# Gated DeltaNet inside a two-layer trunk: the key and query products of a block made once for both directions, and kept in SBUF by ScalarE

## What is computed

```python
# per chunk and head; qn, kn are L2-normalised; forward and backward directions are summed
gc = cumsum(g); decay = exp(where(i >= j, gc_i - gc_j, -inf))
lower = where(i > j, (k_i * b_i) . k_j * decay, 0)         # key x key
sol   = solve(I + lower, [v * b, k * b * exp(gc)])          # u, w
intra = where(i >= j, q_i . k_j * decay, 0)                 # query x key
v_new = u - w S
o     = (q * exp(gc)) S + intra v_new
S     = S * exp(g_last) + (k * exp(g_last - g))^T v_new
# o = o_fwd + flip(o_bwd of the flipped sequence)
```

## Time and profile before

| | |
|---|---|
| median of 3 runs | 2117.73 us (2115.81 to 2118.25) |
| profiled execution, its time | 2117.53 us |
| its span, first to last instruction | 2115.7 us |
| mean granted TensorE clock | 0.969 |
| busy: TensorE / weight load / VectorE / ScalarE / GpSimd | 94% / 88% / 50% / 31% / 21% |
| recurrence of the first layer | about 404 to 537 us |
| recurrence of the second layer | about 1433 to 1566 us |

### The profile page before, as it was taken

One profiled execution on the slowest core, in us unless ns is written; L12 is line 12 of the kernel. 1 busy time (PEld: TensorE's weight loads), 2 busy tenths in 40 slices (PEclk: granted clock), 3 DMA queues, 4 the chain that ended last, 5 costly groups with the idle time before them and its releaser, 6 DMA issues. The chain is left out here.

```text
span 2115.7 us, 33396 instructions
## 1 busy us (share of the span) xinstructions
PE 1990.3 (94%) x14407; PEld 1871.7 (88%) x14407; DVE 1059.3 (50%) x1666; ACT 664.4 (31%) x1009; POOL 446.5 (21%) x326
## 2 busy tenths in 40 slices
PE   5999979899899999999999998898979999999996
PEld 3999957788899999999999988587879999999996
DVE  3445886577652323323455478666775332333232
ACT  2543225412223131312335422552122313122231
POOL 4000010133243030312430000103323412122144
PEclk9999989999899999999999998999989999999998
DMA  8444120100333222122254431101012212221211
GB/s 330 160 161 152 41 66 1 36 1 1 115 131 109 80 100 80 61 80 80 70 201 160 145 108 61 25 2 36 1 55 80 81 64 77 80 80 61 80 61 50
DMA packets 45635, 177.89 MB, mean 84 GB/s; under 512 B 21073, under 2 KB 22865, under 8 KB 26033
## 3 DMA queue, kind: packets, MB, share of 16 engines
q1 hardware_dynamic: 43952, 174.29, 23.5%
q10 hardware_dynamic: 1536, 1.48, 0.2%
HBM read 166.98 MB, written 8.68 MB: 83 GB/s over the span
## 5 line engine op out<-in xcount | busy, mean ns | idle before, releaser
L1416 PE MATMUL PS<-HH,HI 128*128 128x322 f32 (+1 forms) x1792 | 420.4, 316 | 4.5 <-DVE HL L939 4.5
L1416 PE MATMUL PS<-HL,HI 128*128 128x322 f32 (+1 forms) x1792 | 415.2, 313 | 0.0
L1416 PE MATMUL PS<-HH,LO 128*128 128x322 f32 (+1 forms) x1792 | 414.2, 312 | 0.0
L603 ACT CAST HI<-RAW 128x2048 fp32r<-128x2048 f32 x96 | 182.8, 1904 | 514.0 <-PE PS L1416 478.8
L1416 PEld LDWEIGHTS PS<-HH,HI 128*128 128x128 f32 x1792 | 303.3, 191 | 8.8 <-issue 8.7
L1416 PEld LDWEIGHTS PS<-HH,LO 128*128 128x128 f32 x1792 | 306.1, 191 | 0.0
L1416 PEld LDWEIGHTS PS<-HL,HI 128*128 128x128 f32 x1792 | 305.2, 191 | 0.0
L1416 PE MATMUL PS<-FH,HI 128*128 128x320 f32 x1280 | 293.3, 310 | 0.0
L1416 PE MATMUL PS<-FH,LO 128*128 128x320 f32 x1280 | 292.0, 309 | 0.0
L932 DVE TENSOR_TENSOR LO<-RAW,HI 128x2048 fp32r<-128x2048 f32 x96 | 232.6, 2423 | 103.1 <-ACT HI L603 103.1
L1416 PE MATMUL PS<-FL,HI 128*128 128x320 f32 x1152 | 263.6, 310 | 0.0
(11 more groups left out here) (270 smaller groups left out, 2624.2 us busy)
## 6 DMA issues: line engine op xcount, KB each, us to landing
RAW<-ws SPq DMA_DIRECT2D x96, 1024.0 KB, 4.8
ADA<-ada SPq DMA_DIRECT2D x48, 1024.0 KB, 5.0
X<-xT SPq DMA_DIRECT2D x1, 2560.0 KB, 16.4
X<-xT SPq DMA_DIRECT2D x2, 1280.0 KB, 5.7
xs<-X SPq DMA_DIRECT2D x1, 2560.0 KB, 8.8
X<-xs SPq DMA_DIRECT2D x2, 1280.0 KB, 5.7
yT<-YB SPq DMA_DIRECT2D x8, 320.0 KB, 2.2
ROT<-rot SPq DMA_DIRECT2D x2, 1024.0 KB, 4.8
```

The lines of the kernel that those rows point to most:

```text
L603: nc.scalar.copy(HI[g % 2][:, :], RAW[g % 2][:, :]).then_inc(hi_ready, 1)
L1416: last = pe.matmul(bank(2 * u + a)[:, 0:e], w[:, cols], m[:, a, 0:e], start=(k == 0 and f), stop=(k == KT - 1 and e_))
```

## The change

In steps 0 and 1 the products are made for both directions as before, and ScalarE copies each direction's two banks (128x1024) into a new tile `KK[s][d]`; VectorE makes CM and AT from the copy. In steps 2 and 3 no products are made: the block that one direction reaches in step `s` is the one that the other had in step 3 - `s`, so CM and AT are made from `KK[3 - s][1 - d]`. In step 4 the products of the context block are made once (`d` = 0, banks 1 and 2), and both directions read them there in PSUM. The first pair of KK tiles lies where X lies, so the reload of X's first half moves behind the last use of KK (step 3), and the loads of SS stand ahead of it.

```diff
@@ -114,7 +114,7 @@
     pads=3, p_out=PT_, tap=12, taps=12, conv=12, silu=12, csq=8, css=8, crt=2, crr=2, kdm=4, kde=4, kdw=256, kdr=16, gce=2, gcr=128, mke=1, mex=1, wi=2, leaf=1, wst=32, wud=128, crb=8, chat=16,
     msq=3, mss=1, mrt=2, mrr=1, mrb=2, map_=3, vtr=4, vte=4, ktr=4, kte=4,
     g_tr=1, g_cp=1, gate_e=2, gate_b=4, gate_mm=1, gate_t=3, gate_x=6,
-    gb=10, dtm=10, dta=10, eg=10, de=10, dtn=10, keq=16, kk=10, cm=10, atm=10, u1=10, tp=20, tcp=20, pm=20, pe_=20,
+    gb=10, dtm=10, dta=10, eg=10, de=10, dtn=10, keq=16, kk=5, kkc=4, cm=10, atm=10, u1=10, tp=20, tcp=20, pm=20, pe_=20,
     qm=20, um=20, ks=8, xs=10, ym=10, vn=10, vs=8, om=10, oa=10, su=8, sst=8,
     o_rt=2, o_dn=4, rr=5, rot=5, krc=5, pmm=9, pev=9, qrc=4,
     as_=20, amx=20, aex=20, adg=20, apt=20, apc=20, apv=10,
@@ -218,6 +218,8 @@
         UU = two("UU", 7)
         TT, VN = two("TT", 8), two("VN", 8)
         SS = two("SS", 9)
+        KK = [[place(f"KK{s}{d}", [P, H, 2, P], F32, w) for d, w in enumerate(at_)]
+              for s, at_ in enumerate(((r_x, r_x + 4096), (r_t + 10240, r_t + 20480)))]
         KTOK = place("KTOK", [P, H, T], F32, r_split + 2 * KT * CH * 4)
 
         o = r_split
@@ -438,9 +440,11 @@
                                          t["leaf"][d, q].rearrange("n r c -> r n c")).then_inc(S["wud"], 16)
                     sp.wait_ge(S["apv"], o["apv"] + PAIRS)
                     sp.wait_ge(S["bpv"], o["bpv"] + PAIRS)
-                    sp.dma_start(X[:, 0:4, :, :], t["xs"][:, 0:4] if l else t["xT"][:, 0:4]).then_inc(S["xa"], 16)
                     for d in range(2):
                         sp.dma_start(SS[d][:, :, :], t["s0"][l, d]).then_inc(S["s0_in"], 16)
+                    sp.wait_ge(S["cm"], o["cm"] + 2 * LB)
+                    sp.wait_ge(S["atm"], o["atm"] + 2 * LB)
+                    sp.dma_start(X[:, 0:4, :, :], t["xs"][:, 0:4] if l else t["xT"][:, 0:4]).then_inc(S["xa"], 16)
                     sp.wait_ge(S["xlo"], o["xlo"] + H)
                     sp.dma_start(X[:, 4:KT, :, :], t["xs"][:, 4:KT] if l else t["xT"][:, 4:KT]).then_inc(S["xb"], 16)
                     refill(g0 + 12)
@@ -832,13 +836,19 @@
                     turned_k(2)
                     turned_k(3)
                     for s in range(NB):
+                        if s < 2:
+                            for d in range(2):
+                                act.wait_ge(S["kk"], o["kk"] + 2 * s + d + 1)
+                                nc.scalar.copy(KK[s][d][:, :, :, :].rearrange("p h q c -> p (h q c)"),
+                                               PS[:, 4 * d + 1:4 * d + 3, :].rearrange("p a b -> p (a b)")
+                                               ).then_inc(S["kkc"], 1)
                         for n in range(NL):
                             for d in range(2):
                                 act.wait_ge(S["tp"], o["tp"] + (s * NL + n) * 2 + d + 1)
                                 nc.scalar.copy(TT[d][:, :, :],
                                                bank(4 * d + 3).rearrange("p (h c) -> p h c", h=H)).then_inc(S["tcp"], 1)
                             if n == 0 and s == LB:
-                                act.wait_ge(S["kk"], o["kk"] + 2 * NB)
+                                act.wait_ge(S["kk"], o["kk"] + 5)
                                 act.wait_ge(S["keq"], o["keq"] + 4 * LB)
                                 for j in range(H):
                                     for g in range(2):
@@ -1230,9 +1240,13 @@
                         blk = blocks[s]
                         for d in range(2):
                             v = 2 * s + d
-                            dve.wait_ge(S["kk"], o["kk"] + v + 1)
+                            if s < LB:
+                                dve.wait_ge(S["kkc"], o["kkc"] + min(v + 1, 4))
+                                kkq = (KK[s][d] if s < 2 else KK[3 - s][1 - d])[:, :, :, :]
+                            else:
+                                dve.wait_ge(S["kk"], o["kk"] + 5)
+                                kkq = PS[:, 1:3, :].rearrange("p a (h q c) -> p (a h) q c", h=2, q=2)
                             dve.wait_ge(S["dtn"], o["dtn"] + v + 1)
-                            kkq = PS[:, 4 * d + 1:4 * d + 3, :].rearrange("p a (h q c) -> p (a h) q c", h=2, q=2)
                             if s:
                                 dve.wait_ge(S["su"], o["su"] + (2 * s if s < LB else 2 * (LB - 1)))
                             nc.vector.tensor_tensor(CM[d][:, :, :], kkq[:, :, 1, :], DTB[d][:, :, :],
@@ -1713,9 +1727,9 @@
                     for s in range(NB):
                         blk = blocks[s]
                         prev = s > 0
-                        for d in range(2):
-                            if prev:
-                                pe.wait_ge(S["oa"], o["oa"] + 2 * s)
+                        if prev:
+                            pe.wait_ge(S["oa"], o["oa"] + 2 * s)
+                        for d in range({0: 2, 1: 2, LB: 1}.get(s, 0)):
                             pe.wait_ge(S["eg"], o["eg"] + 2 * s + d + 1)
                             for h in range(H):
                                 o_ = bank(4 * d + 1 + h // 2)[:, (h % 2) * 256:(h % 2) * 256 + 256]
@@ -1745,7 +1759,9 @@
                                 i = (s * NL + n) * 2 + d
                                 pe.wait_ge(S["pe_"], o["pe_"] + i + 1)
                                 if n == 0:
-                                    pe.wait_ge(S["atm"], o["atm"] + 2 * s + d + 1)
+                                    pe.wait_ge(S["atm"], o["atm"] + 2 * s + 2)
+                                    if s < 2:
+                                        pe.wait_ge(S["kkc"], o["kkc"] + 2 * s + 2)
                                 for h in range(H):
                                     last = pe.matmul(bank(4 * d + 1)[:, toks(h)], PP[d][:, h, :], UU[d][:, h, :],
                                                      start=True, stop=True)
```

## The result

| | before | changed |
|---|---|---|
| median | 2116.43 us (2115.69 to 2118.25, 6 runs) | 2125.31 us (2123.11 to 2127.13, 6 runs) |
| ratio, 95% interval | | 1.0041 [1.0028, 1.0054] |
| span of the profiled execution | 2115.7 us | 2125.2 us |
| mean granted TensorE clock | 0.969 | 0.963 |
| recurrence, first and second layer (first DT to DNSQ) | 132.09 / 133.18 us | 135.40 / 135.41 us |

The account below looks back on a forecast made before the run. It took a slackless chain at each step's start, not TensorE's 94% busy time, as the bound. Terms 0.5 + 1.15 - 0.4 + 0.95 - 1.5 gave +0.7 us a layer, +1.4 for two: 2119.1 us, range 2113 to 2123.

Parts of the forecast that it names:

- forecast of no change: Whole kernel: measured time within 0.2%, or 4.2 us, of before, from 2113.5 to 2122.0 us; chance 0.69.
- Slower by over 0.2%: Whole kernel: above 2122.0 us, taking most of rival B and a tail; chance 0.17.
- rival B: Step 3's start: TensorE, idle 2.4 us for CM1, drops to 1.2 GHz, some 1.6 us lost a layer; 2122.1 us; chance 0.17.
- rival C: TensorE is the bound: five groups of 1.81 us a layer come off, 18.1 us, giving 2100.6 us; chance 0.02.
- starts of steps 0, 1, 3 and 4: Time to each step's first PP, per layer: +0.5 us (copies), +1.15 and +0.95 (turns), -1.5 (fewer products).
- The turns of VectorE and GpSimd: Steps 1 to 3: reading SBUF, both engines alternate whole instructions, about 1.7 us a pair.
- The moved loads: X reload after step 3 and earlier SS loads: costed at nothing; X transfer's 5.7 us if the cover were gone.
- Rival A: CM and AT from KK run beside GpSimd without turns: -4.2 and -3.65 us for the layers, 2109.8 us; chance 0.10.
- clock 1.00 through step 3: Sign in the changed profile: TensorE keeps its full clock in step 3; 0.5 after its start would mean rival B.
- +0.7 for the rest: Sum of the five steps' terms in the recurrence, +0.7 us a layer, with no clock drop.
- step 2, "-0.4 us": Time to step 2's first PP: products gone, GpSimd's QE holds VectorE once; -0.4 us a layer.
- what follows the recurrence: Time between the recurrence and the output projection: no change; a change there would show the prediction wrong.

Follow-up runs that it names:

- number 2: Changed kernel with four unread products added on TensorE in steps 2 and 3, between the two directions' products; 2114.94 us, ratio 0.9990 to the kernel before.
- number 3: Kernel before with only the loads moved as in the change (SS first, X's first half after step 3); 2117.06 us, ratio 0.9998.
- number 1: Changed kernel, with GpSimd starting KE and QE in steps 1 to 3 only after CM and AT of both directions; 2109.05 us, ratio 0.9967 to before.
- numbers 10 and 11: Kernel before with one and three more VectorE instructions ahead of CM in step 0 of the first layer; ratios 0.9992 and 0.9997.
- number 12: Same program as number 1 run once more (changed kernel, GpSimd's KE and QE waiting for CM and AT); 2110.58 us, ratio 0.997 to before.
- number 11: Kernel before with three more VectorE instructions ahead of CM in step 0 of the first layer; ratio 0.9997.
- number 9: Kernel before, unchanged, profiled once more; ratio 0.9997.

## Why the prediction was wrong

**The side.** The forecast of no change (0.69) fell. Slower by over 0.2% had 0.17, with rival B behind it, and B is what happened, larger.

**What held.** TensorE's 94% was no bound: with products put back the kernel is faster (number 2), and rival C's 2100.6 was out of reach. The starts of steps 0, 1, 3 and 4 came at +0.52, +1.07, +0.92 and -1.60 against +0.5, +1.15, +0.95 and -1.5. The turns of VectorE and GpSimd cost what had been counted from the earlier trace rows. The moved loads are free (number 3). Rival A's price for a layer without turns, 4.2 us, was near the 4.4 of number 1, with two terms missing that about cancel (+1.2 and -1.3).

**The step that failed first: "clock 1.00 through step 3".** The clock was left out of the sum and given to a rival of 0.17. It falls twice in a layer, in steps 2 and 3, in both layers and both profiles. B weighed one wait of 2.4 us in step 3 against one of 3.04 that had made it fall and one of 1.7 that had not the earlier trace rows. B's own mechanism failed as well: the wait for CM1 that it blamed begins only after the fall in seven of eight places. Ahead of the fall stand 1.36 to 1.39 us for the state update and 0.52 for CM0, with 1.06 us of work between them, and each of these waits is shorter than the one of 1.7 that the earlier trace rows shows to be harmless. In the kernel before 3.62 us of products stood there, and these the change took away. So idle times were weighed one by one, where the work around them was what the change took away: TensorE is busy 1.32 us of the three ahead of the fall, against 3.00 before. The removed products and the turns act together as far as these runs show: number 1 has the products gone and keeps 1.00 without the turns, and number 2 has the turns, with products put into the wait for CM1, keeps 1.00 in three of the four places and has before's recurrence time again. A rule that tells such places beforehand does not follow from these runs: number 1 is idle for more than half of 466 to 469 and keeps 1.00.

**The second: B's size.** B took 1.6 us a layer for one fall. The falls cost 1.50 and 1.63 in the first layer; by number 2 against the changed kernel it is 3.1 in the second. With +0.7 for the rest, two falls in each of two layers would have given 2117.7 + 1.4 + 6.4 = 2125.5, which is the result. (B's 2122.1 starts from the profiled 2117.53; from the median, as the other rivals do, it is 2122.3.) That agreement is partly luck, because of the next two points, and because the median of before, measured beside the result, is 2116.4: from there the sum is 2124.2.

**The third: step 2, "-0.4 us".** Its start was +0.62 in the first layer and +1.72 in the second, since GpSimd's phase was read from rows that the change itself moves. The compensation, -1.35 and -2.43 at the end of step 1, was not foreseen either: there the clock no longer falls behind the idle time of the earlier trace rows, though TensorE waits the same 2.85 us for VN. Together they make -0.7 against the forecast -0.4.

**The fourth: what follows the recurrence was taken as unchanged.** The median rose by about 9 us, the recurrences by 5.5 to 6.8. The rest lies between them: the same TensorE work, done with more time at 1.2 GHz (the rows above show it, not its cause). Whether the change adds it by its timing stays open: the attempt to shift the phase by itself (numbers 10 and 11) did not shift it.

## What to carry to other kernels

An operand moved from PSUM to SBUF puts VectorE among the readers that take turns with GpSimd; look at what GpSimd's queue holds at that moment, and if it has slack, let it wait, as two lines did here for 16 us. Work taken from TensorE in a part where it waits for others saves only what the next wait leaves of it (at step 3's start nothing with the turns, 1.9 us without) and can cost its clock: before removing it, look at what is left between two waits, not at the longest wait alone, and try the change with the removed work put back as a control. Cost every edit by the piece from one landmark to the next, with the clock beside it, since here four correct terms were outweighed by falls of the clock that the sum had no term for.

## What the runs showed of the hardware that was not expected

More work made the kernel faster: products whose results nobody reads (four matmuls in each of two steps and two layers, sixteen in all) took 10 us off the changed kernel, 5.4 of them in the recurrences; that the other 4.7 are their doing is not shown. The clock fell behind waits of 1.4 and 0.5 us with 1.06 us of work between them. It did not fall behind the wait of 2.85 us for VN at the end of step 1 in the changed kernel, where it fell behind the same wait in the kernel before. And it is not the same in every execution of a program: number 12 falls at 1487, number 1 does not, and number 11's second recurrence takes 130.0 us instead of 132.2, with nothing changed in that layer; the difference there lies ahead of PP of step 0 (12.86 us instead of 15.06 in number 9), where number 9 is at 0.50 from 1441 to 1444 us and number 11 at 1.00. A difference of 1 or 2 us between two single profiles of such a kernel is thus no evidence; the pieces that repeat in every layer are.
